# Weight pages stored as four planes of 2 KB rows and gathered with four runs per partition

## The reference, cut to what matters

```python
mod = silu_c @ w_mod + b_mod                      # 1024 x 6144
h = modulate(rms_norm(x, norm1_w), sh1, sc1)
q, k, v, g, f = split_proj(h @ w_in)              # 1024 x 3584; retention and a Fourier branch follow
x = x + g1 * merge_branches(...)
x = x + g2 * conv_ffn(h2, w_up, conv_w, conv_b, w_down)   # 1024 x 5632 and 2816 x 1024
...                                               # second block: RWKV-7 and mLSTM branches
# PEER: 16384 experts, 8 heads x 16 experts chosen for each token
s = einsum('nhpc,hpkc->nhpk', q, sub_keys);  s_top, i_top = top_k(s, 16)
best, pos = top_k(cand, 16);  gate = softmax(best)
act = gelu(einsum('tkd,td->tk', u_emb[expert], tok)) * gate
out = einsum('tk,tkd->td', act, v_emb[expert])    # u_emb, v_emb: 16384 x 1024 each
```

## Time and profile before

| what | us |
|---|---|
| median of two runs | 1979.2 (1978.57 and 1979.84) |
| the profiled execution, device time | 1980.98 |
| the same execution, span of its profile | 1979.1 |
| TensorE busy | 1584.2 (80%) |
| VectorE busy | 1060.6 (54%) |
| ScalarE busy | 721.9 (36%) |
| GpSimd busy | 517.5 (26%) |

### The profile page before, as it was taken

One profiled execution on the slowest core, in us unless ns is written; L12 is line 12 of the kernel. 1 busy time (PEld: TensorE's weight loads), 2 busy tenths in 40 slices (PEclk: granted clock), 3 DMA queues, 4 the chain that ended last, 5 costly groups with the idle time before them and its releaser, 6 DMA issues.

```text
span 1979.1 us, 31231 instructions
## 1 busy us (share of the span) xinstructions
PE 1584.2 (80%) x12072; PEld 1453.2 (73%) x12072; DVE 1060.6 (54%) x1902; ACT 721.9 (36%) x1009; POOL 517.5 (26%) x395
## 2 busy tenths in 40 slices
PE   8999999999999998997999999800000029999998
PEld 4999789999999987896999999700000018888887
DVE  5666567776577846576444444300000018888887
ACT  2434455664467533312444444300000003333333
POOL 0010000331000120056455555566565640000000
PEclk9999999999999999998999999955555559999999
DMA  8864145985443302343655665411111136666664
GB/s 308 322 257 169 65 150 193 341 322 215 145 160 133 145 25 101 116 126 107 193 190 173 187 183 178 106 0 0 0 0 0 0 89 243 244 243 242 242 240 164
DMA packets 95401, 312.61 MB, mean 158 GB/s; under 512 B 42576, under 2 KB 59088, under 8 KB 59856
## 3 DMA queue, kind: packets, MB, share of 16 engines
q1 hardware_dynamic: 52832, 271.60, 38.6%
q0 software_dynamic: 41472, 33.70, 9.0%
q10 hardware_dynamic: 1008, 6.05, 0.8%
HBM read 293.36 MB, written 17.96 MB: 157 GB/s over the span
## 4 chain that ended last, share of the span: by engine, by line
PE 50%; POOL 22%; issue 17%; DVE 6%; ACT 3%; DMA 1%; POOLq 0%; DVEq 0%; SPq 0%; ACTq 0%
PE ps L507 50%; POOL gate_table L479 21%; DVE piece L1686 1%; POOL arena L463 1%; POOL arena L469 1%; ACT piece L1211 1%; DMA ring<-in_stream 1%; DMA arena<-in_xT 0%; DVE arena L1736 0%; ACT arena L1250 0%; DVE arena L1789 0%; ACT arena L1569 0%; ACT L1246 0%; DVE arena L1753 0%; DVE arena L1806 0%
## 5 line engine op out<-in xcount | busy, mean ns | idle before, releaser
L1211 ACT ACTIVATE piece<-ring 128x1024 fp32r<-128x1024 f32 x432 | 452.8, 1056 | 812.6 <-PE ps L507 461.7
L1686 DVE TENSOR_TENSOR piece<-ring,piece 128x1024 fp32r<-128x1024 f32 x432 | 531.7, 1239 | 382.1 <-ACT piece L1211 380.6
L507 PE MATMUL ps<-h_r,piece 128*128 128x256 f32 x5616 | 683.2, 284 | 4.7 <-DVE piece L1686 3.7
L507 PEld LDWEIGHTS ps<-h_r,piece 128*128 128x128 f32 x5616 | 676.8, 192 | 10.8 <-issue 9.1
L507 PE MATMUL ps<-piece,late_r 128*128 128x512 f32 x1536 | 351.0, 391 | 345.6 <-DVE late_r L2477 345.6
L507 PEld LDWEIGHTS ps<-piece,late_r 128*128 128x128 f32 x1536 | 290.1, 189 | 406.3 <-DVE late_r L2477 345.8
L479 POOL DMA_INDIRECT gate_table<-early x256 | 410.3, 1603 | 322.1 <-issue 322.1
L2473 DVE TENSOR_TENSOR early<-early,arena 128x256 f32<-128x256 f32 x128 | 53.5, 418 | 347.3 <-DMA early<-gate_table 347.3
L1238 ACT ACTIVATE arena<-ps 128x256 f32 (+2 forms) x171 | 73.5, 431 | 211.9 <-PE ps L507 211.9
L507 PE MATMUL ps<-arena,ring 128*128 128x256 f32 x512 | 115.7, 387 | 13.3 <-ACT arena L1238 11.7
L507 PEld LDWEIGHTS ps<-arena,ring 128*128 128x128 f32 x512 | 98.8, 195 | 28.1 <-ACT arena L1238 12.5
(11 more groups left out here) (299 smaller groups left out, 1457.6 us busy)
## 6 DMA issues: line engine op xcount, KB each, us to landing
ring<-in_stream SPq DMA_DIRECT2D x240, 1024.0 KB
arena<-in_mod POOLq DMA_DIRECT2D x16, 1024.0 KB, 5.9
gate_table<-early POOLq DMA_DIRECT2D x16, 1024.0 KB, 9.0
early<-gate_table SPq DMA_DIRECT2D x64, 256.0 KB, 4.4
gate_table<-early POOLq DMA_INDIRECT x256
arena<-in_const ACTq DMA_DIRECT2D x1, 2256.0 KB, 10.6
arena<-in_const ACTq DMA_DIRECT2D x1, 1648.0 KB, 8.7
xres<-in_xT SPq DMA_DIRECT2D x1, 1024.0 KB, 4.9
```

The costliest lines, as they stand in the source:

```text
L507: mm_last[0] = nc.tensor.matmul(*args, **kw)
L1211: A(piece[:, 0, c % 3], ring[:, p % RING, s], ACT.Copy).then_inc(S["hi_ready"], 1)
L1686: TT(piece[:, 1, c % 3], ring[:, p % RING, s], piece[:, 0, c % 3].bitcast(F32), ALU.subtract).then_inc(S["lo_ready"], 1)
```

## The change

The host lays each page out as four planes of 128 rows of 2 KB: plane a holds the a-th quarter of every partition's 8 KB. The transfer of a page names four runs of 2 KB for each partition, 256 KB apart in HBM, and puts them side by side in the same 8 KB of the ring slot. Bytes, number of transfers, waits and everything that reads the ring stay as they are.

```diff
         @block.sync
         def _(sp):
             def page(p, i=0):
-                sp.dma_start(ring[:, p % RING], t["stream"][p + RING * i]).then_inc(loaded[p % RING], 16)
+                sp.dma_start(ring[:, p % RING].rearrange("p s k m -> p s (k m)").rearrange("p s (a n) -> p (s a) n", a=2),
+                             t["stream"][p + RING * i].rearrange("a p n -> p a n")).then_inc(loaded[p % RING], 16)
...
     for k, block in enumerate(blocks):
         stream[n + k // 2, :, 1024 * (k % 2):1024 * (k % 2 + 1)] = block
+    stream = stream.reshape(NPAGES, P, 4, 512).transpose(0, 2, 1, 3)
```

## The result

The changed kernel takes 2014.5 us (two runs, 2012.0 and 2017.0) for 1979.2 before: 35 us slower, ratio 1.018 [1.012, 1.023]. Measured once more beside other kernels it gives 1.023 [1.020, 1.026]. The forecast was 1986, its upper end 1999.

A forecast was written before the change was run, and what follows sets the result against it. TensorE, then POOL's scatters, then TensorE were taken to bound the kernel. From the profiled 1981.0 us, +1.2 at the start and +6 in the scatters gave 1988.2, less 1.8 to the median: 1986 us, range 1948 to 1999 (likeliest case 1980 to 1994).

The forecast's parts named there:

- What bounds the kernel, and where pages touch the end: TensorE, then POOL's 256 scatters, then TensorE set the end; pages touch it for 13 us at the start and through scatters.
- Packets: Page transfers: 512 packets a page instead of 128, so queue q1 goes from 52832 to 144992.
- Issue on SP: SP's issue of a page takes some 480 ns, +0.15 us for each of 240, hidden outside the start.
- Time of a packet: Four 2 KB runs take 7% longer than one of 8 KB (0 to 11%), so a page grows by 0.18 us.
- At the start: Two page waits on the path, 13.0 us, grow by 0.9 us and two issues by 0.3: +1.2 us (0 to +2).
- In the scatter stage: POOL's scatters beside the pages: 35 held scatters each wait 0.18 us longer, together +6 us (0 to +12).
- The rival of scatters getting in between the runs: Scatters' packets alternate with 2 KB runs, one a page, 53 us for 70, or half delayed; 1955 us, chance 0.32.
- the 70: In the scatters' stretch, 70 us of the span were reckoned as what scatters lose to pages in the kernel before.
- The slower rival: Runs 256 KB apart slow HBM, pages hold engines much longer, losses grow in proportion: 2021 us, chance 0.08.

The follow-up runs named there:

- e3: Four planes only for the 56 pages of the u stage, beside the scatters, the other 184 as in the kernel before: +1.7% to the kernel before.
- e4: Four planes for all pages but the 56 of the u stage, against the kernel before: +0.3%.
- e12: The changed kernel with its four planes timed once more against the kernel before: ratio 1.023 [1.020, 1.026].
- e1: Four runs of 2 KB a partition as in the changed kernel, each padded with 256 bytes to lie within 9 KB of HBM: as slow as the changed kernel.
- e5: All pages in eight planes of 128 rows of 1 KB, 1024 packets a page, against the kernel before: +2.4%.
- e2: Pages in two planes of 128 rows of 4 KB, two runs a partition, against the kernel before: +0.4%.
- e13: Layout of before; SP issues each u-stage page only after two more scatters have been issued: 1980.4 us, 0.5% slower than the kernel before.
- e16: Four planes for all pages, and SP issues each u-stage page only after three more scatters: 2012.5 us, for 1994.9 with the layout of before so paced.
- e6: Kernel before, but u-stage page transfers move only the first 1 KB of each partition's 8 KB, in one run: ratio 0.985.

## Why the prediction was wrong

- *What bounds the kernel, and where pages touch the end.* Right: TensorE's windows unchanged, last stage 360.6 for 360.8 us, and the loss where POOL's scatters meet the pages (e3 against e4).
- *Packets.* 144992 as forecast. *Issue on SP*: a median of 373 ns, not 480; the line through 333 and 383 ns didn't hold. It hides as forecast.
- *Time of a packet.* 447 packets of 0.91 MB for 128 of 1.02 MB in 3.2 us, with shares of 80.6% and 84.9%: 0.0923 us for 2 KB against 0.340 for 8 KB, 9% more (6% for data packets alone, 92.7 and 350 ns), within my 0 to 11%. Right as an average, and beside the point: a scatter needs all 16 engines, and the page's last packet is 0.45 (e12) to 0.66 us later where I put 0.18; a held scatter waits 4.40 us on the mean for 3.47. **This is the step that failed first**: "A page's moving time of 8 x 0.328 = 2.6 us grows by 0.18 us (0 to 0.29)", and from it "a held scatter waits 0.18 us longer". It took the mean over engines for the slowest. The rows of 1 KB and 2 KB runs that I relied on come from transfers with 8 or 16 runs an engine; the late last packet appears with 32 (e1, e12, changed) and 64 (e5) and not with 16 (e2).
- *At the start*: +1.2 us forecast. In the chain of the changed kernel, which has four page transfers where there were two, the block of matmuls starts at 58.96 instead of 53.89 us. The columns are as in the earlier trace rows:

```profile
1.38 9.70 DMA ring<-in_stream
...
16.54 5.60 DMA ring<-in_stream
...
22.54 7.71 DMA ring<-in_stream
...
36.36 6.83 DMA ring<-in_stream
...
58.96 61.04 PE ps L508 x506
```

  5.1 us, of which 3.8 are left at the first scatter. But this pair is at the far ends: that block starts between 53.6 and 56.8 us in seven other kernels whose first pages have runs of 8 KB, and between 55.2 and 58.1 in seven others with runs of 2 or 1 KB there. With the pair the means are 2.1 us apart, and the first scatter starts at 858.6 to 863.3 and at 858.1 to 862.9 us, no clear difference. So some 2 us are the layout's, not 5. That the late last packet makes them, because each of these pages is waited for whole, is likely and not shown.
- *In the scatter stage*: +6 us forecast, 32.6 measured, from two errors of like size. The waiting grew by 15.6 us: as many scatters are held as I reckoned (28 to 31, I put 35), and each waits 0.9 us longer where I put 0.18. And "what a held scatter waits" was taken as the only cost: the writing stood in no term and grew by 16.8 us, 1.65 to 1.85 us a scatter in the pages' stretch, because 38 of them for 10 had to wait for the rest of a subtraction on VectorE. The scatters' row of before, with 2607 ns as its longest beside a median of 1562, would have told of it. The scatters and the pages are two loops that move against each other, and a shift of some tenths of a microsecond decided where in VectorE's work the scatters start.
- *The rival of scatters getting in between the runs* (0.32) did not occur: held scatters still waited 4.40 us on the mean, and POOL went on some 1.0 us behind the page's last packet with 8, 16, 32 and 64 runs an engine. The Trainium skill's page "DMA: Bandwidth & Descriptors", section "Queues, rings and completion order", would have it so by its ceiling of 64 descriptors for a packet, and not by its typical 9 to 17. The traces here speak against the typical size for these transfers; they don't show where a packet ends.
  Two readings of that rival were loose: equal counts of packets (81 to 80) don't show that they alternated one to one, and half of 53 us off the 70 leaves 43 less, not 45.
- *The slower rival* (0.08, 2021 us) had the right place and nearly the right size, by the wrong mechanism: HBM rows 256 KB apart have no part (e1). Its rule that the loss grows in proportion to the hold doesn't hold either: a last packet later by a tenth to a seventh (0.45 to 0.66 of 4.46 us) cost half of the 70 us again.

What is open: why the last packets come late from 32 runs an engine on (they look like one engine's, but the traces don't name engines), why the longer hold moves the scatters' starts from the last moments of VectorE's subtractions into their midst (it did so in e1, e3, e5 and e12 as well, but nothing here forecasts it), and why the pages' stretch gains from two pieces of 2 KB runs but not from two of 4 KB. No run moved VectorE's subtraction or took it away; that the writing waits for it rests on 4205 scatters in 18 traces, not on an experiment of its own.

No variant here is faster than the kernel before with all its bytes moved.

## What to carry to other kernels

A transfer that nobody waits for can still set the time, if another queue's small transfers on the end's path stand behind it: cost it by its last packet on the slowest engine, not by bytes over mean rate. And where two loops share engines without a common clock, a few tenths of a microsecond in one can move the other by more than the sum of the delays; look at the spread of the affected instruction (1547/1562/2607 ns here), not at its median, and give the range for it. Before you put a long instruction down to something that happens near it, lay every engine's timeline beside it, and test the rule in a kernel where the two candidates come apart: SP's page issue and VectorE's subtraction keep a nearly fixed distance in most of the kernels here, and only e13 to e16 tell them apart.

## What the runs showed of the hardware

- With 8 or 16 runs an engine a 1 MB transfer's last packet ends 4.5 to 4.6 us after its issue; with 32 or 64 runs at 4.9 to 5.2 us, while nine tenths of its packets are in at 4.2 to 4.5 us (4.2 to 4.3 with 8 or 16).
- Where a scatter's packets stand behind a page, their last ends 0.07 us behind the page's last packet, and GpSimd starts the next scatter some 1.0 us behind it, with 8, 16, 32 and 64 runs an engine (0.99, 1.01, 1.04, 1.08).
- SP's issue of a transfer takes hardly longer for more runs: 333 ns for 128, 373 for 512.
- An indirect transfer's descriptor writing on GpSimd takes 1.56 us alone. If it starts while VectorE subtracts one SBUF tile from another (1.23 us, 128x1024 float32), it takes 1.56 us plus the rest of that subtraction less 0.12: up to 2.6 us. Pages of 128 KB change nothing in that (37 long ones in e6).
- 512 packets of 256 bytes cost the other queue no more than 128 of 1 KB (1942.4 and 1942.1 us).
